# Sums of a seven-product matmul moved from GpSimd to VectorE, and its first products spread over the block before

## The reference

```
up = einsum('btd,de->bte', h, w_in)            # 1024 -> 2 x 2816
conv = conv_b + conv_w[0] * padded[:, 0:T] + ...  # width 3 along the frames
u, gate = split(conv, 2)
y = einsum('btf,fd->btd', silu(gate) * u, w_out)  # 2816 -> 1024
```

## Time and profile before

| | |
|---|---|
| median of three runs | 1386.44 us |
| profiled execution | 1385.95 us, span 1384.2 us |
| TensorE busy | 1363.6 us (99%) |
| VectorE busy | 1033.7 us (75%) |
| ScalarE busy | 690.5 us (50%) |
| GpSimd busy | 210.8 us (15%) |
| up chunk 1 to the third group's end | about 1052 to 1360 us of the span |

### The profile page before, as it was taken

One profiled execution on the slowest core, in us unless ns is written; L12 is line 12 of the kernel. 1 busy time (PEld: TensorE's weight loads), 2 busy tenths in 40 slices (PEclk: granted clock), 3 DMA queues, 4 the chain that ended last, 5 costly groups with the idle time before them and its releaser, 6 DMA issues.

```text
span 1384.2 us, 26540 instructions
## 1 busy us (share of the span) xinstructions
PE 1363.6 (99%) x10776; PEld 1283.9 (93%) x10776; DVE 1033.7 (75%) x1694; ACT 690.5 (50%) x1554; POOL 210.8 (15%) x224
## 2 busy tenths in 40 slices
PE   9999999999999999999999999999999999999999
PEld 6888888999999999999988888889899999999999
DVE  5688677479888788678765746576897887878885
ACT  5543434466553354252565655645665553563550
POOL 0000000200000000000400000001200543342540
PEclk9999999999999999999999999999999999999999
DMA  9654542344445443535333323113244223222222
GB/s 380 242 175 144 181 150 84 102 150 132 159 145 168 175 160 131 182 119 191 122 143 107 132 94 115 64 63 122 92 138 138 84 69 96 88 92 92 77 80 96
DMA packets 38017, 182.44 MB, mean 132 GB/s; under 512 B 4294, under 2 KB 6854, under 8 KB 26632
## 3 DMA queue, kind: packets, MB, share of 16 engines
q1 hardware_dynamic: 22984, 126.98, 26.4%
q0 software_dynamic: 14912, 53.78, 11.2%
HBM read 172.82 MB, written 7.91 MB: 131 GB/s over the span
## 4 chain that ended last, share of the span: by engine, by line
PE 84%; DVE 8%; ACT 3%; issue 3%; DMA 1%; POOL 0%; SPq 0%; DVEq 0%; ACTq 0%; POOLq 0%
PE ps L819 24%; PE ps L821 24%; PE ps L820 24%; DVE w_lo L1974 2%; PE ps L1285 2%; PE ps L1335 1%; DVE cv L2475 1%; PE ps L1244 1%; DVE t_lo L2007 1%; PE ps L1307 1%; PE ps L1078 1%; PE ps L1074 1%; ACT cv L1789 1%; PE ps L1065 1%; DVE xT L2183 1%
## 5 line engine op out<-in xcount | busy, mean ns | idle before, releaser
L821 PE MATMUL ps<-h_hi,w_lo 128*128 128x272 f32 x2048 | 592.9, 289 | 0.0
L819 PE MATMUL ps<-h_hi,w_hi 128*128 128x272 f32 x1952 | 569.9, 292 | 7.4 <-ACT up L1732 4.4
L820 PE MATMUL ps<-h_lo,w_hi 128*128 128x272 f32 x1952 | 562.0, 288 | 0.0
L821 PEld LDWEIGHTS ps<-h_hi,w_lo 128*128 128x128 f32 x2048 | 385.6, 188 | 0.0
L819 PEld LDWEIGHTS ps<-h_hi,w_hi 128*128 128x128 f32 x1952 | 368.1, 189 | 17.6 <-issue 10.9
L820 PEld LDWEIGHTS ps<-h_lo,w_hi 128*128 128x128 f32 x1952 | 368.6, 189 | 1.0 <-issue 1.0
L1974 DVE TENSOR_TENSOR w_lo<-w_raw,w_hi 128x2048 fp32r<-128x2048 f32 (+3 forms) x96 | 200.5, 2089 | 53.7 <-ACT w_hi L1397 52.8
L1397 ACT CAST w_hi<-w_raw 128x2048 fp32r<-128x2048 f32 (+3 forms) x97 | 162.1, 1676 | 134.9 <-PE ps L821 107.9
L2183 DVE SCALAR_TENSOR_TENSOR xT<-ps,ada,xT 128x272 f32<-128x272 f32 (+2 forms) x288 | 107.1, 408 | 66.5 <-PE ps L821 65.9
L819 PE MATMUL ps<-act_hi,w_hi 128*128 128x274 f32 (+1 forms) x524 | 152.2, 290 | 1.1 <-ACT ps L1430 0.8
L820 PE MATMUL ps<-act_lo,w_hi 128*128 128x274 f32 (+1 forms) x524 | 151.6, 289 | 0.0
(11 more groups left out here) (329 smaller groups left out, 2274.1 us busy)
## 6 DMA issues: line engine op xcount, KB each, us to landing
w_raw<-in_wst SPq DMA_DIRECT2D x72, 1024.0 KB, 4.8
a_raw<-in_ada_r POOLq DMA_DIRECT2D x56, 512.5 KB, 4.3
w_raw<-in_wst SPq DMA_DIRECT2D x28, 768.0 KB, 4.3
a_raw<-in_ada_g POOLq DMA_DIRECT2D x24, 512.0 KB, 3.6
a_pro<-in_ada_p SPq DMA_DIRECT2D x8, 1024.0 KB, 16.6
v_raw<-in_wst SPq DMA_DIRECT2D x8, 1024.0 KB, 8.1
w_raw<-in_wst SPq DMA_DIRECT2D x10, 512.0 KB, 4.4
xT<-in_xT SPq DMA_DIRECT2D x4, 544.0 KB, 5.2
```

The costliest lines, as they stand in the source:

```text
L819: mm(out, lhs_hi, rhs_hi, start=first, stop=False, skip_group_check=skip)
L820: mm(out, lhs_hi, rhs_lo, start=False, stop=False, skip_group_check=skip)
L821: return mm(out, lhs_lo, rhs_hi, start=False, stop=last, skip_group_check=skip)
```

## The change

The activation sums leave GpSimd: `act_sums` goes, and `act_sum(c, part)` does the same eight instructions on VectorE in three parts of 3, 2 and 3, each behind the conv of an up tile (`SUMS_AT`): for the first two groups (2,0), (2,1), (3,0), for the third (0,1), (1,0), (1,1). For the first two groups the splits of the sums move one tile on: 1 and 3 to (3,1), 2 and 4 to (4,0).

TensorE's order at a group's opening becomes: up units (0,0), (0,1), product 1, up unit (1,0), products 5 and 2, up unit (1,1), products 6 and 3; what follows is as before. A22 is split before A11, one tile earlier than so far for the first block; the casts of S4 for the first block come in (4,1) (third group (2,1)) instead of the closing block. The seed copy goes ahead of `head_in` of the closing block's tile 1; the A22 cast of the second block goes behind the act_hi cast of its tile 0. VectorE evacuates products 5, 2, 6 before the last conv, 3 and 7 after it.

```diff
-SEVEN_HEAD = [(0, 5), (0, 2), (0, 6), (0, 3)]
+SEVEN_HEAD = [(0, 6), (0, 3)]
...
-        UNITS += [(_b, 0, 0), (_b, 0, 1), (_b, 1, 0), (_b + 1, 1, None), (_b, 1, 1)]
+        UNITS += [(_b, 0, 0), (_b, 0, 1), (_b + 1, 1, None), (_b, 1, 0), (_b + 1, 5, None), (_b + 1, 2, None), (_b, 1, 1)]
...
-        for p in (5, 6, 2, 7, 3):
+        for p in (5, 2, 6, 3, 7):
...
-SUM_SPLITS = {(1, 1, 3, 0): (1, 3), (1, 1, 3, 1): (2, 4), (1, 2, 3, 0): (1, 3), (1, 2, 3, 1): (2, 4), (1, 3, 1, 1): (1, 3), (1, 3, 2, 0): (2, 4)}
+SUMS_AT = {(1, c, 2, 0): 0 for c in (1, 2)}
+SUMS_AT.update({(1, c, 2, 1): 1 for c in (1, 2)})
+SUMS_AT.update({(1, c, 3, 0): 2 for c in (1, 2)})
+SUMS_AT.update({(1, 3, 0, 1): 0, (1, 3, 1, 0): 1, (1, 3, 1, 1): 2})
+SUM_SPLITS = {(1, c, 3, 1): (1, 3) for c in (1, 2)}
+SUM_SPLITS.update({(1, c, 4, 0): (2, 4) for c in (1, 2)})
+SUM_SPLITS.update({(1, 3, 1, 1): (1, 3), (1, 3, 2, 0): (2, 4)})
...
             # GpSimd
-            def act_sums(c):
...
-            for c in range(3):
-                act_sums(c)
-                for i in range(4):
-                    weight_sums(GROUPS[c] + i)
+            for name in SEVEN:
+                weight_sums(BN[name])
...
             # TensorE
-                            units(us[0:3])
+                            units(us[0:2])
                             product(n + 1, 1)
+                            unit(us[2])
+                            product(n + 1, 5)
+                            product(n + 1, 2)
                             unit(us[3])
...
             # ScalarE, per up tile
+                            if closing and t == 1:
+                                seed(n + 1)
                             if BL[n] not in PAIR_OF:
                                 head_in(u0, t, l, tile)
...
-                            if closing and t == 0:
-                                split_sums(n + 1, ("S4",))
-                            if closing and t == 1:
-                                seed(n + 1)
                             act.wait_ge(unit_done, u1 + 1)
                             if closing and t == 1:
                                 split_both(n + 2)
-                                split_a22(n + 2)
+                                split_sums(n + 2, ("S1",))
...
                             elif t == 1 and n + 2 in GROUPS:
-                                split_seven(n + 2)
+                                split_both(n + 2)
+                                split_sums(n + 2, ("S1", "S3", "S2", "S4"))
+                            elif t == 0 and n + 2 in GROUPS:
+                                split_a22(n + 2)
...
                                 act.copy(act_hi[:, c % 2, 2 * (b // 2) + t, :], cv[:, 0, t, :]).then_inc(act_hi_ok, 1)
+                                if closing and t == 0:
+                                    split_a22(n + 2)
...
             # VectorE
+            def act_sum(c, part):
...
+                if part == 0:
...
+                    step.then(TT(whole(3), hi(0, 0), lo(0, 0), ALU.add))
+                    step.then(TT(whole(1), whole(3), hi(0, 1), ALU.subtract))
+                    TT(whole(1), whole(1), lo(0, 1), ALU.subtract).then_inc(t_sum_ok, 1)
+                elif part == 1:
+                    step.then(TT(whole(2), hi(1, 0), lo(1, 0), ALU.add))
+                    TT(whole(3), whole(2), whole(3), ALU.subtract).then_inc(t_sum_ok, 1)
+                elif part == 2:
+                    dve.wait_ge(t_sum_ok, 4 * c + 2)
+                    TT(whole(2), whole(2), whole(1), ALU.subtract).then_inc(t_sum_ok, 1)
+                    dve.wait_ge(t_sum_ok, 4 * c + 3)
+                    step.then(TT(whole(4), hi(1, 1), whole(2), ALU.subtract))
+                    TT(whole(4), whole(4), lo(1, 1), ALU.add).then_inc(t_sum_ok, 1)
...
                         seven_out(n, 2)
+                        low_seven(n + 1, "A22")
+                        low_seven(n, "S3")
                         low_seven(n + 1, "A11")
-                        low_seven(n, "S3")
-                        low_seven(n + 1, "A22")
...
                             if closing and t == 1:
...
+                                seven_out(n + 1, 5)
+                                seven_out(n + 1, 2)
                                 low_seven(n + 2, "A11")
-                                seven_out(n + 1, 5)
-                                low_seven(n + 2, "A22")
+                                seven_out(n + 1, 6)
+                                low_seven(n + 2, "S1")
...
+                            if (l, c, b, t) in SUMS_AT:
+                                act_sum(c - 1, SUMS_AT[(l, c, b, t)])
...
                             elif closing:
-                                seven_out(n + 1, 6)
-                                seven_out(n + 1, 2)
-                                low_seven(n + 2, "S1")
+                                seven_out(n + 1, 3)
                                 low_seven(n + 2, "A12")
```

More of the change, by code:

```diff
@@ L588, in hybrid_stream_step @@
         s_sum_ok, s_hi_ok, s_lo_ok, seeded = sem("s_sum_ok"), sem("s_hi_ok"), sem("s_lo_ok"), sem("seeded")
-        t_step, t_sum_ok, t_hi_ok, t_lo_ok = sem("t_step"), sem("t_sum_ok"), sem("t_hi_ok"), sem("t_lo_ok")
+        t_sum_ok, t_hi_ok, t_lo_ok = sem("t_sum_ok"), sem("t_hi_ok"), sem("t_lo_ok")
         lam_ok, lam_exp = sem("lam_ok"), sem("lam_exp")
@@ L768, in _ @@
                 row_load(n)
-            step = Steps(pool, t_step)
             ptt = pool.tensor_tensor
-            def act_sums(c):
[L774 to L791, removed]
             def weight_sums(n):
@@ L804, in weight_sums @@
                 pool.wait_ge(s_sum_ok, 4 * k + 3)
-                pool.wait_ge(s_lo_ok, 5 * k + 2)
+                pool.wait_ge(s_lo_ok, 5 * k + 1)
                 ptt(raw_("S4"), raw_("A12"), raw_("S2"), ALU.subtract).then_inc(s_sum_ok, 1)
-            for c in range(3):
-                act_sums(c)
-                for i in range(4):
-                    weight_sums(GROUPS[c] + i)
+            for name in SEVEN:
+                weight_sums(BN[name])
         @block.tensor
@@ L1158, in product @@
                             mm(ps[:, SEVEN_BANKS[i]["b"], 0:HALF + 2], h_hi[:, 0, 0:P], h_hi[:, 0, 0:HALF + 2], start=True, stop=True)
-                    pe.wait_ge(s_lo_ok, 5 * k + 1)
+                    pe.wait_ge(s_lo_ok, 5 * k + 2)
                     bank_free(u)
@@ L1402, in split_both @@
                 act.wait_ge(unit_done, slots_done(HI_PREV[n]) + 1)
-                slot, count = loaded_at(n)
-                act.wait_ge(w_in[slot], count)
                 act.copy(hi_cols(n, 0, 2 * QC), low_cols(w_raw, n, 0, 2 * QC)).then_inc(s_hi_ok, 1)
@@ L1408, in split_a22 @@
                 k = SEVEN_K[n]
+                slot, count = loaded_at(n)
+                act.wait_ge(w_in[slot], count)
                 if k >= 3:
@@ L1420, in split_seven @@
             def split_seven(n):
+                split_a22(n)
                 split_both(n)
-                split_a22(n)
                 split_sums(n, ("S1", "S3", "S2"))
@@ L1794, in ffn @@
                             if t == 1 and closing:
-                                split_sums(n + 2, ("S1", "S3", "S2"))
+                                split_sums(n + 2, ("S3", "S2"))
                             elif t == 1 and n + 2 in GROUPS:
-                                split_seven(n + 2)
+                                split_both(n + 2)
+                                split_sums(n + 2, ("S1", "S3", "S2", "S4"))
+                            elif t == 0 and n + 2 in GROUPS:
+                                split_a22(n + 2)
                             elif t == (0 if BL[n] in PAIR_OF else 1):
@@ L1980, in low_seven @@
                 if part == "A11":
-                    dve.wait_ge(s_hi_ok, 5 * k + 1)
+                    dve.wait_ge(s_hi_ok, 5 * k + 2)
                     dve.wait_ge(s_sum_ok, 4 * k + 2)
@@ L1984, in low_seven @@
                 elif part == "A22":
-                    dve.wait_ge(s_hi_ok, 5 * k + 2)
+                    dve.wait_ge(s_hi_ok, 5 * k + 1)
                     if k >= 3:
@@ L2002, in low_seven @@
                     TT(seven_lo(n, "S3"), seven_extra(s_raw, n, "S3"), f32(seven_hi(n, "S3")), ALU.subtract).then_inc(w_lo_ok, 1)
+            def act_sum(c, part):
+                hi = lambda kh, half: f32(act_part(act_hi, c, kh, half))
+                lo = lambda kh, half: f32(act_part(act_lo, c, kh, half))
+                whole = lambda i: t_raw[i][:, :, :]
+                if part == 0:
+                    if c:
+                        dve.wait_ge(unit_done, LAST_U[GROUPS[c - 1] + 3] + 1)
+                    else:
+                        dve.wait_ge(arow_ok, ROWS_DONE)
+                    dve.wait_ge(act_ok, FT + C0[c] + CH[c])
+                    step.then(TT(whole(3), hi(0, 0), lo(0, 0), ALU.add))
[10 more added lines that the diff above has]
+                    TT(whole(4), whole(4), lo(1, 1), ALU.add).then_inc(t_sum_ok, 1)
```

(8 more changed lines are left out.)

1 line of the change is left out of this document (removed).

## The result

The changed kernel takes 1402.65 us (median) against 1386.57 us for the kernel before: a ratio of 1.011, 95% interval 1.009 to 1.013. That median is over four runs, of which three took 1400.42, 1402.44 and 1402.87 us and one, a slow one that the ratio leaves out, 7462.68 us. It is slower, as forecast, but by 16 us where 6 were forecast, and outside the range. The profiled execution has a span of 1400.7 us.

What follows compares the result with a forecast made beforehand. TensorE was taken as the bound, time won or lost only in its pauses. Groups +1.65, +4.45, +2.6 and −2.55 behind product 2 gave +6.1 on 1385.95: 1392.1, or 1392.5 us on the median's scale; range 1384.5 to 1397.5.

Steps and rivals of the forecast that it cites:

- G: Moment ScalarE starts again after act_hi of tile (3,1) (second group); forecast to move −1.65, +1.15, +1.0 us by group.
- order, and G to product 2 (head): At each group's opening, up to product 2: lost cover plus the changed seed chain; forecast +3.3, +3.3, +1.6 us.
- behind product 2: TensorE's pauses after product 2 in each group: forecast net −0.85 us per group, range −1.5 to 0.
- the direction: Whole kernel: slower by more than 2.8 us, given 71%.
- the 3.0 us of lost cover: At product 2: 3.0 us of TensorE work per group that covered the seed now comes after it.
- From G to product 2: Chain leading to the seed and product 2: forecast +0.3 us in the first two groups, −1.4 in the third.
- ending ScalarE's wait for S4: On ScalarE before product 2: a wait of 1.29 us idle goes, because A22's low comes a tile earlier.
- the clock: Rival: product 2's pause is the long one, the next up unit runs at 1.2 GHz; +4.4 us, 1396.5, 12%.
- Product 7's 1.3 us: Pause at product 7 of each group's first block, waiting for product 6's evacuation; forecast to go, 1.3 us per group.
- block 1's product 2: The next block's product 2 waits for A12's low after the last up unit; forecast +0.3 us.
- block 2's product 1: In the third block, A11 follows A22 and S3 without product 7's pause as cover; forecast +0.35 us.

Runs made afterwards that it cites:

- the narrow sums: Weight sums S1, S2, S4 done on 32 of 384 columns, rest left out: in the changed kernel 1388.19 us, in the kernel before 1377.07 us.
- e4: The changed kernel with TensorE's pauses before products 1 and 5 filled with matmuls of no use; 1401.19 us, ratio 1.0104 to the kernel before.
- e3: The changed kernel with the closing block's seed copy right behind up tile (5,0) on ScalarE; 1396.24 us, ratio 1.0067 to the kernel before.
- e2: The changed kernel with the activation sums back on GpSimd, new TensorE order and early A22 cast kept; 1396.65 us, ratio 1.0075 to the kernel before.

## Why the prediction went wrong

By the table, with the forecast's terms regrouped:

| term | forecast (group 1, 2, 3) | measured |
|---|---|---|
| G (ahead) | −1.65, +1.15, +1.0 | −1.6, +1.1, +1.2 |
| order, and G to product 2 (head) | +3.3, +3.3, +1.6 | +5.8, +4.3, +4.3 |
| behind product 2 | −0.85 each | +0.4 each |

**Right: the direction, and G.** The sums on VectorE took 1.01 to 1.02 us (forecast 1.0) where nothing disturbed them; the three of part 2 in the third group, beside GpSimd's weight sums, took 1.71 to 1.84. The pauses ahead of the group went and came as said: none at 1090, a new one of 0.96 at 1228.81, 3.41 at 1320.08. The pauses at product 1 and product 2 are there, behind the instructions named.

**Right in kind: the 3.0 us of lost cover.** With the narrow sums the heads lose 2.6, 2.8 and 1.2 us more than before, near the +3.3, +3.3 and +1.6 of the forecast. That bears the price per group out, though no run changes the order and nothing else.

**Failed: "From G to product 2", put at +0.3.** Forecast 15.7 us in all groups, measured 16.7 in all three:
```profile
1113.73 0.38 ACT L1718 COPY up<-ps 128x272 f32<-128x272 f32 x1
...
1129.89 0.38 ACT L1416 COPY ps<-ps 128x274 f32<-128x274 f32 x1
```
(product 2 at 1130.41). So the term was +1.3 in the first two groups. I followed the chain on ScalarE and took VectorE's share as unchanged. VectorE had 2.8 us to spare in front of the closing tile's conv: that conv began 2.84 us after VectorE fell idle. After, VectorE comes to it 3.9 us later, counted from G (10.4 us after G instead of 6.5), and ScalarE, which feeds it, 0.2 us later. The slack is used up, and the conv of (5,0) at 1124.09 starts without a rest, some 0.85 us late. The 3.9 us are, to 0.2, the moved pair (1.93) and a contention of 2.2 us in the conv of (4,1) and A11's and S1's lows (1.42, 1.35 and 1.36 for 0.79, 0.55 and 0.55). Neither alone exceeds the slack. A22's low, and the contention in the conv of (5,0) itself (1.54 for 0.79 in its first half), add next to nothing, since they stood in this stretch before too (kernel before, second group):
```profile
1227.85 0.55 DVE L1988 TENSOR_TENSOR s_lo<-w_raw,w_third 128x384 fp32r<-128x384 f32 x1
...
1232.54 1.42 DVE L2476 SCALAR_TENSOR_TENSOR cv<-up,vec,cv 128x546 f32<-128x546 f32 x1
```
A22's early cast, which I credited with ending ScalarE's wait for S4, brings the S4 sum to the middle of this queue: GpSimd's row at 1119.60 is released by A22's low. I had listed all these instructions and put them to product 1's account alone; they delayed the seed too. With narrow sums the way from G to product 2 is 15.0 us in the first group, and VectorE rests 0.31 us before that conv (row at 1122.47):
```profile
1113.02 0.38 ACT L1719 COPY up<-ps 128x272 f32<-128x272 f32 x1
...
1128.05 0.37 PE L803 MATMUL ps<-act_hi,w_hi 128*128 128x274 f32 x1 [0.79 <-ACT ps L1417]
```
ScalarE waits for no sum of GpSimd on this way, wide or narrow, so the missing 1.0 us is gone with the contention. That the pair is needed for it as well follows from the sum above and is not shown by a run. The 1.0 us appears three times in the table, 1.0 us per group: the filled kernel's heads, free of the clock, stand 4.3, 4.3 and 2.6 over before.

**Failed: the clock, put at nothing in the sum and at 12% as a rival.** It was part of the outcome: 1.5 and 1.7 us of the first and third head, by e4. I had argued that product 2's own pause would be short since product 1's is long. Both were near 2 us in the first group, and in the third product 2's was the longer (1.89 against 1.17): product 1's start moves everything behind it but does not bring the seed nearer, because act_hi was late by its own chain.

**Failed: "Behind product 2", put at −0.85, measured +0.4.** Product 7's 1.3 us went, as said, and the two losses that I priced came near their size: block 1's product 2 +0.4 (forecast +0.3), block 2's product 1 +0.4 (+0.35). Not foreseen were 0.73 at product 4 of block 0 and 0.37 at product 1 of block 3, 1.1 us per group. The rows at 1142.38 and 1144.37 show the first: the gate product took 1.53 for 0.72 beside GpSimd, and the evacuation of product 7 (1143.83) stands behind it on VectorE. With narrow sums both waits are gone. The forecast had contention in A12's low alone and did not follow VectorE's queue further on.

These three are 3 x 1.0, some 3 and 3 x 1.27: the 10 us between 6 and 16.

## What to carry to other kernels

Before a consumer is moved earlier, follow back not only the engine that ends last but also the one with slack beside it, and subtract everything that the change puts into that slack, contention included; a wait of 2.8 us on the second engine was all the room there was. Work that another engine triggers (here GpSimd's S4 sum, by A22's low) moves with its trigger, so ask what it will then stand beside. Where several queue moves each shift the same 2 us to the next product, look at the sum of the engine's work instead of its order: in the kernel before, narrowing GpSimd's sums brought 9 us (leaving work out), and the best of the orders tried here 2.

## What the runs showed of the hardware that was not expected

Whether a pause of TensorE is followed by the 1.2 GHz level is not told by its length. Product 1's pause of 2.16 us in the changed kernel was not followed by it, one of 2.15 in e3 was, with the same work of TensorE and the same pause (0.97 and 0.96 us) in front of both. A pause of 1.88 us at product 2 was followed by it in the changed kernel (0.66 over 1131 to 1136), one of 1.90 at the same place with the sums back (e2) was not; there the pause at product 1 had been 0.40 instead of 2.16. The windows of the changed kernel, e3 and e2, and the rows of the last two:
```profile
1122.00:1131.00 9.00, 6.19 (x47) 6.00 (x48) 8.25 (x11) 3.52 (x10) 3.02 (x4) 1.00 0.00 0
...
1125.00:1130.00 5.00, 5.00 (x30) 5.00 (x29) 4.96 (x7) 1.03 (x2) 1.58 (x2) 0.66 0.00 0
...
1131.00:1136.00 5.00, 5.00 (x42) 5.00 (x42) 1.08 (x5) 0.90 (x2) 1.01 (x1) 1.00 0.01 1
...
1124.56 0.39 PE L802 MATMUL ps<-act_hi,w_hi 128*128 128x274 f32 x1 [2.15 <-DVE w_lo L1972]
...
1130.62 0.36 PE L820 MATMUL ps<-act_hi,w_hi 128*128 128x274 f32 x1 [1.90 <-ACT ps L1434]
```
Where it came in these heads, an up unit lost 0.8 to 1.5 us. What decides is open here; that busy work in the pause kept the level in the first and third head is shown by e4.
